# Forgetting attention on one core: TensorE multiplies the values of two units in one stretch in every second step

## The reference

```
def _fox_attention(q, k, v, c):      # (B,H,S,d); c: cumulative log forget gates
    ...
        s = jnp.einsum('bhqd,bhkd->bhqk', qb, k) * scale + (cb[..., :, None] - c[..., None, :])
        mask = k_pos[None, :] <= q_pos[:, None]
        p = jax.nn.softmax(jnp.where(mask, s, MASK_VALUE), axis=-1)
        return jnp.einsum('bhqk,bhkd->bhqd', p, v)
```

## Time and profile before

| | us |
|---|---|
| median of 3 runs | 1349.88 |
| lowest and highest run | 1349.45, 1350.01 |
| profiled execution | 1350.16 |
| its span, first to last instruction | 1348.1 |
| TensorE busy in the span | 1334.4 (99%) |
| VectorE, ScalarE, GpSimd busy | 454.5, 480.0, 529.8 |
| granted TensorE clock, mean | 0.999 |

### The profile page before, as it was taken

One profiled execution on the slowest core, in us unless ns is written; L12 is line 12 of the kernel. 1 busy time (PEld: TensorE's weight loads), 2 busy tenths in 40 slices (PEclk: granted clock), 3 DMA queues, 4 the chain that ended last, 5 costly groups with the idle time before them and its releaser, 6 DMA issues.

```text
span 1348.1 us, 17988 instructions
## 1 busy us (share of the span) xinstructions
PE 1334.4 (99%) x6943; PEld 1092.7 (81%) x6943; DVE 454.5 (34%) x857; ACT 480.0 (36%) x759; POOL 529.8 (39%) x421
## 2 busy tenths in 40 slices
PE   9999999999999999999999999999999999999997
PEld 7888877788888888888787877677898888888886
DVE  4364446771111111011643554545621111110105
ACT  3413266533222223211365554644332222222120
POOL 4422433334444444543352332323244444435440
PEclk9999999999999999999999999999999999999999
DMA  6301121314333332323123212313133333333221
GB/s 213 123 32 63 63 94 63 95 38 119 95 94 94 95 101 90 137 94 109 47 84 94 63 33 63 95 63 95 32 110 110 94 94 94 94 109 107 107 84 63
DMA packets 141540, 119.55 MB, mean 89 GB/s; under 512 B 5808, under 2 KB 120720, under 8 KB 141456
## 3 DMA queue, kind: packets, MB, share of 16 engines
q1 hardware_dynamic: 141216, 118.10, 27.9%
q10 hardware_dynamic: 240, 0.31, 0.1%
HBM read 116.20 MB, written 2.10 MB: 88 GB/s over the span
## 4 chain that ended last, share of the span: by engine, by line
PE 96%; DVE 2%; issue 1%; ACT 0%; DMA 0%; POOL 0%; SPq 0%; DVEq 0%; ACTq 0%; POOLq 0%
PE banks L561 28%; PE banks L563 28%; PE banks L562 28%; PE banks L989 2%; PE banks L1132 2%; PE banks L1167 2%; PE banks L1148 1%; PE banks L674 1%; PE banks L1080 1%; PE banks L1007 1%; PE banks L1067 1%; PE banks L1140 1%; PE banks L1118 0%; DMA x_res<-in_x_dram 0%; PE banks L1094 0%
## 5 line engine op out<-in xcount | busy, mean ns | idle before, releaser
L1281 POOL TENSOR_TENSOR w_lo<-w_raw,w_hi 128x512 fp32r<-128x512 f32 x417 | 529.6, 1299 | 786.9 <-ACT w_hi L1328 523.7
L561 PE MATMUL banks<-xT_lo,w_hi 128*128 128x512 f32 (+2 forms) x1024 | 383.7, 375 | 0.9 <-DVEq L1688 0.7
L563 PE MATMUL banks<-xT_hi,w_hi 128*128 128x512 f32 (+2 forms) x1024 | 380.0, 371 | 0.0
L562 PE MATMUL banks<-xT_hi,w_lo 128*128 128x512 f32 (+2 forms) x1024 | 379.9, 371 | 0.0
L1328 ACT ACTIVATE w_hi<-w_raw 128x2048 fp32r<-128x2048 f32 (+1 forms) x106 | 198.2, 1869 | 174.5 <-PE banks L563 145.6
L561 PEld LDWEIGHTS banks<-xT_lo,w_hi 128*128 128x128 f32 (+1 forms) x1024 | 191.4, 187 | 35.7 <-issue 3.3
L563 PEld LDWEIGHTS banks<-xT_hi,w_hi 128*128 128x128 f32 (+1 forms) x1024 | 191.3, 187 | 34.0
L562 PEld LDWEIGHTS banks<-xT_hi,w_lo 128*128 128x128 f32 (+1 forms) x1024 | 191.5, 187 | 32.6
L1960 DVE TENSOR_TENSOR banks<-silu_g,banks 128x512 f32<-128x512 f32 x44 | 30.6, 696 | 402.3 <-PE banks L563 402.3
L561 PE MATMUL banks<-w_lo,xT_hi 128*128 128x512 f32 (+1 forms) x352 | 135.9, 386 | 1.6 <-ACT q_raw L1350 0.7
L561 PE MATMUL banks<-w_lo,hT_hi 128*128 128x512 f32 x352 | 137.1, 390 | 0.0
(11 more groups left out here) (196 smaller groups left out, 1214.6 us busy)
## 6 DMA issues: line engine op xcount, KB each, us to landing
w_raw<-in_ffn_w_dram SPq DMA_DIRECT2D x92, 512.0 KB, 4.4
w_raw<-in_ffn_w_dram SPq DMA_DIRECT2D x20, 1024.0 KB, 4.9
w_raw<-in_even_w_in_dram SPq DMA_DIRECT2D x13, 1024.0 KB, 4.8
w_raw<-in_fox_w_in_dram SPq DMA_DIRECT2D x16, 512.0 KB, 4.4
w_raw<-in_fox_w_in_dram SPq DMA_DIRECT2D x8, 1024.0 KB, 5.6
w_raw<-in_even_w_out_dram SPq DMA_DIRECT2D x4, 1024.0 KB, 4.9
w_raw<-in_fox_w_out_dram SPq DMA_DIRECT2D x4, 1024.0 KB, 4.9
x_res<-in_x_dram SPq DMA_DIRECT2D x4, 512.0 KB, 7.1
```

Of the source, the lines that this page charges most:

```text
L561: mm(acc, l_hi, r_lo, start=first, stop=False)
L562: mm(acc, l_lo, r_hi, start=False, stop=False)
L563: return mm(acc, l_hi, r_hi, start=False, stop=final)
L1281: ins = nc.gpsimd.tensor_tensor(w_lo[c % RING][:, a:a + n], w_raw[c % RAW][:, a:a + n], w_hi[c % RING][:, a:a + n].bitcast(F32), ALU.subtract)
```

## The change

Before, TensorE multiplied the values of unit s - 3 in step s, from step 3 on. Now a function gives the units whose values come in a step: in an even step from 4 to 30 the units s - 4 and s - 3, one directly behind the other, in an odd step up to 29 none, and in the steps 31 to 34 one unit each as before.

```
+            def values_of(s):
+
+                if s >= F_UNITS - 1:
+                    return [s - 3]
+                return [s - 4, s - 3] if s >= 4 and s % 2 == 0 else []
+
...
                 if 2 <= s < F_UNITS + 2:
                     turn_pair(s - 2)
-                if s >= 3:
-                    pair_values(s - 3)
+                for u in values_of(s):
+                    pair_values(u)
```

## The result

| | before | changed |
|---|---|---|
| median of the runs, us | 1349.8 | 1353.88 |
| lowest and highest run | 1349.45, 1350.11 | 1353.19, 1355.97 |
| ratio, with its 95% interval | | 1.0033 (1.0022 to 1.0044) |
| profiled execution | 1350.16 | 1354.66 |
| its span | 1348.1 | 1352.6 |

Each kernel has six runs here. The changed kernel is slower by 4.1 us, in the range and 0.7 us above the forecast. The slowest of its six runs, 1355.97 us, has the lowest mean granted clock on record, 0.996 against 0.998 in four of the six.

A forecast was written before the change was run, and what follows sets the result against it. TensorE's queue was taken to bound the kernel, 1334.4 of 1348.1 us busy. Waits of 7.9 us less a gain of 4.6 gave +3.3, 1353.5 on the profiled execution and 1353.2 us for the median; range 1349.2 to 1356.2.

The forecast's parts named there:

- The gain: TensorE enters and leaves the values 14 times less, at 0.33 us each: 4.6 us gained.
- nothing is saved: Rival: the fixed 0.33 us belongs to each unit and stays, so only the waits are left: 1357.8 us; chance 0.05.
- step 10: Second piece behind it: TensorE waits 1.5 us for the bank that ScalarE's late `q_raw` copy holds.
- steps 6 and 14: The transpose of a heads tile waits for bank 3, 0.5 us each, 1.0 us together.
- step 18: As at the heads-tile transposes waiting for bank 3, with sums of squares in VectorE's chain as well: 1.4 us wait.
- step 19: TensorE arrives 0.55 us earlier without its values, but the copy it waits for is no earlier: 0.55 us given back.
- step 20: Late sums of squares: TensorE waits 2.3 us at the scores of step 21, about 0.4 at the transposes behind.
- small ones: Waits at the tile transpose of step 22, the scores of step 8 and the last transposes: 0.3, 0.15, 0.3 us.
- The rule weighed: VectorE's norms collide with GpSimd's subtraction on the shared port pair: not in the sum; as rival 1355.5 to 1356, chance 0.07.
- the gain comes through: Rival: TensorE's reserve covers the late chains, banks are free in time; over 2.7 us faster, 1345.3 with no waits; chance 0.08.
- waits and gain balance: Rival: the waits are only 4 to 7 us, no change to be seen, around 1351.3 us; chance 0.33.
- What would show it: Signs: 28 records in one stretch, TensorE waits of 1.5, 1.4 and over 2 us, VectorE idle until L1167.

The follow-up runs named there:

- e1: The changed kernel, but VectorE waits for a unit's values only where it has a bank to move (every fourth unit, and the last pair): 1346.03 us, ratio 0.9972.
- e4: The changed kernel, but with the values of units 16 and 17 singly in steps 19 and 20 as before: 1349.82 us, ratio 1.0001 to the kernel before.
- e3: The kernel before, but with the values of units 16 and 17 together in step 20, all other units as before: 1354.38 us, ratio 1.0038.
- e6: The changed kernel, with ScalarE's table load moved from ahead of the exp of step 20 to behind the copy of that step: 1353.55 us.

## Why the prediction came out

**The gain: right, 0.3 us small.** 14 x 0.33 = 4.6 was forecast, 14 x 0.35 = 4.9 is read. The choice of the upper end held: the part that does not depend on the number of records is paid once for two units. The rival that nothing is saved is out.

**The waits: right in cause and nearly in each place.**

| place | forecast | read |
|---|---|---|
| step 10 | 1.5 | 1.62 |
| steps 6 and 14 | 1.0 | 1.39 |
| step 18 | 1.4 | 1.49 |
| step 19 | 0.55 | 0.54 |
| step 20 | 2.3 + 0.4 | 2.66 + 0.28 |
| small ones | 0.75 | 0.18 |
| sum | 7.9 | 8.16 |

The forecast took starts of TensorE in the trace of before and chains of durations behind one release, and these held to 0.2 us at each place but the scores of step 21, where 2.3 was reckoned and 2.66 read: that chain took 5.9 us (857.17 to 863.11) in place of 5.6, with a read of the accumulator behind the exp (0.19) that the sum had left out. That the total is only 0.3 off is luck in part: 0.6 more at step 20 and 0.4 more at the steps 6 and 14 stand against 0.6 less at the small ones. These were over-estimated: only the scores of step 8 were late; at the tile transpose of step 22, and at the end of the attention, the bank was free in time. Perhaps the chains had caught up there while TensorE was late behind step 20; no run tests this.

**The term that was missing: the clock.** The sum had nothing for what TensorE's idling does to TensorE itself. Behind the wait of 2.6 us the granted clock stood at 0.50 for some 3.4 us, which cost 1.59. With the forecast's own terms 7.9 - 4.6 = 3.3; with 0.3 more of waits, 0.3 more of gain and 1.6 of clock it is the 4.9 that the attention grew by in the profiled executions. The runs' medians differ by 4.1, so the forecast was 0.7 low by these; it came so near although a term of 1.6 us was missing, and how much of that term is in the runs without a trace is open.

**The rule weighed.** At the released place of step 10 the two norms took 1.82 us, and in `e1` at the same place 0.74. In the changed kernel GpSimd's subtraction runs beside them, in `e1` it is nearly over:

```profile
779.96 2.54 POOL L1287 TENSOR_TENSOR w_lo<-w_raw,w_hi 128x512 fp32r<-128x512 f32 x2 [20.39 <-DVE qn L2008]
```

against, in `e1`,

```profile
776.07 2.50 POOL L1287 TENSOR_TENSOR w_lo<-w_raw,w_hi 128x512 fp32r<-128x512 f32 x2 [19.17 <-DVE qn L2008]
```

So the norm is held until about the end of the subtraction (779.96 + 2.54 = 782.50): of the two in the row above the first takes 1.43 us and ends at 782.64, the second takes 0.35. The Trainium skill (SBUF — State Buffer, on the shared port pair) has the loser fully blocked, and the trace agrees. But as the forecast put it, the norm is on none of the chains: ScalarE's `q_raw` comes from the max and the exp, and the wait at step 10 is 1.62 with the collision and was 1.5 by a sum without it. None of TensorE's waits in the changed kernel is put down to the norm. Its price in time is none that can be seen; no run takes the collision away by itself.

**The other rivals.** That the gain comes through was refuted for the changed kernel by its waits of 8.2 us, and is what happens in `e1`, where the reserve suffices. That waits and gain balance is what happens in `e4`, without step 20; the forecast's decision between this and a clear loss hung on that place, and `e3` shows it so.

**What would show it.** The 28 records, the waits behind 10 and 18, the one over 2 us at the scores of step 21, and VectorE standing until L1167 were all seen. Two marks were named wrongly. The stretch was put at 1.65 + 0.15 = 1.80 us to the next piece and read 1.68; by the prediction's own 0.055 us a record it would have been 28 x 0.055 + 0.15 = 1.69. And 0.14 us from two transposes to a piece can't be seen in an odd step, since these have four or eight transposes; the same 0.18 us less was seen there as 0.36 for 0.54.

## What to carry to other kernels

Before work on one engine is moved later, list who waits for its signal, also those who take nothing from it: a wait written "to be in step" costs nothing until its signal comes late, and then it holds all that is queued behind it, on its engine and the next ones. Here one line turned a loss of 4.1 us into a gain of 3.8 us. A forecast can be summed place by place from starts and durations of the trace before, but where it lets TensorE, if that is the engine that bounds the kernel, stand at one place as long as here (2.17 to 3.02 us), it should also hold a term for the half clock behind it.

## What was not expected of the hardware

The half clock came at single waits of 2.17, 2.27, 2.6 (`e3` and the changed kernel, twice each) and 3.02 us, and never at waits of 1.4 us or less, several of which stand in each of these traces. In the changed kernel some 3.4 us of work ran at 1.2 GHz then, at a price of 1.6 us; three waits with the same sum of 2.75 us cost nothing of the kind (`e6`). These are the cases of this kernel, no rule for where the border lies.
